# Where the tensors of a two-block transformer kernel begin in SBUF: weight units 64 bytes off multiples of 128

## What is computed

```python
def modulated_residual(x, c, g, w_mod, b_mod, fn):
    shift, scale, gate = ada_params(c, w_mod, b_mod)      # silu(c) @ w_mod + b_mod
    h = rms_norm(x, g) * (1 + scale) + shift
    return x + gate * fn(h)

def swiglu(h, w_gate, w_up, w_down):
    return (jax.nn.silu(h @ w_gate) * (h @ w_up)) @ w_down

def moe_swiglu(h, w_router, w_gate, w_up, w_down):
    logits = jnp.einsum('bsd,de->bse', h, w_router)
    top_val, top_idx = lax.top_k(logits, TOP_K)            # 2 of 8 experts
    top_w = jax.nn.softmax(top_val, axis=-1)
    gates = jnp.sum(jax.nn.one_hot(top_idx, 8) * top_w[..., None], axis=-2)
    for e in range(8):
        out = out + gates[..., e:e + 1] * swiglu(h, w_gate[e], w_up[e], w_down[e])
    return out
```

## The kernel before

| tensor | start mod 128 |
|---|---|
| `x_tokens`, `x_normed`, `hT_high`, `hT_low`, `table` | 0 |
| `act`, `aT_high`, `aT_low`, `gate_bc` | 0 |
| `mod_acc`, `mod_in`, `raw_units`/`units_low`, `units_high` | 0 |
| `router_high_low`, `qkv`, `qkT`, `masks`, `prob`, `moe_sum`, `y_high`, `y_low`, `scatter_hot` | 96 |

## Time and profile before

### The profile page before, as it was taken

One profiled execution on the slowest core, in us unless ns is written; L12 is line 12 of the kernel. 1 busy time (PEld: TensorE's weight loads), 2 busy tenths in 40 slices (PEclk: granted clock), 3 DMA queues, 4 the chain that ended last, 5 costly groups with the idle time before them and its releaser, 6 DMA issues.

```text
span 2088.6 us, 29232 instructions
## 1 busy us (share of the span) xinstructions
PE 1956.6 (94%) x9196; PEld 1613.7 (77%) x9196; DVE 1639.9 (79%) x2173; ACT 1138.5 (55%) x1616; POOL 36.1 (2%) x47
## 2 busy tenths in 40 slices
PE   2999999989899999999999999988899999789998
PEld 1987888867688888888888888766778888677886
DVE  6988886757798888888888989896676669666554
ACT  1434444443677767776776777654444444545443
POOL 2000000000000000000000000000000000000000
PEclk9999999977899999999999999987699999779999
DMA  8867996545599999999999999947368875735662
GB/s 297 328 242 265 342 357 196 146 153 180 188 359 333 359 329 368 328 365 327 349 346 341 354 338 354 346 159 215 120 211 267 272 234 151 238 116 177 213 217 74
DMA packets 368361, 551.08 MB, mean 264 GB/s; under 512 B 35715, under 2 KB 292998, under 8 KB 368230
## 3 DMA queue, kind: packets, MB, share of 16 engines
q1 hardware_dynamic: 365280, 547.81, 77.3%
q10 hardware_dynamic: 2118, 1.46, 0.2%
q0 software_dynamic: 832, 0.30, 0.1%
HBM read 548.39 MB, written 1.08 MB: 263 GB/s over the span
## 4 chain that ended last, share of the span: by engine, by line
PE 83%; DVE 10%; ACT 3%; issue 3%; DMA 1%; POOL 0%; DVEq 0%; ACTq 0%; POOLq 0%
PE ps L401 23%; PE ps L403 23%; PE ps L402 23%; PE ps L877 3%; PE ps L866 2%; DVE units_low L396 2%; PE ps L1046 2%; PE ps L931 2%; DVE mod_acc L1546 1%; PE ps L728 1%; PE ps L854 1%; DVE x_tokens L1573 1%; ACT prob L1239 1%; DVE x_normed L1572 1%; DMA mod_in<-in_mod_w 1%
## 5 line engine op out<-in xcount | busy, mean ns | idle before, releaser
L396 DVE TENSOR_TENSOR units_low<-raw_units,units_high 128x1024 fp32r<-128x1024 f32 (+2 forms) x840 | 983.0, 1220 | 121.9 <-ACT units_high L392 115.7
L392 ACT ACTIVATE units_high<-raw_units 128x1024 fp32r<-128x1024 f32 (+2 forms) x840 | 845.0, 1058 | 244.3 <-PE ps L403 232.8
L401 PE MATMUL ps<-units_high,hT_high 128*128 128x512 f32 (+2 forms) x1576 | 624.1, 396 | 4.3 <-DVE act L1642 2.9
L402 PE MATMUL ps<-units_low,hT_high 128*128 128x512 f32 (+2 forms) x1576 | 621.3, 394 | 0.0
L403 PE MATMUL ps<-units_high,hT_low 128*128 128x512 f32 (+2 forms) x1576 | 621.0, 394 | 0.0
L401 PEld LDWEIGHTS ps<-units_high,hT_high 128*128 128x128 f32 (+1 forms) x1576 | 297.4, 189 | 75.8 <-DVE act L1642 3.6
L403 PEld LDWEIGHTS ps<-units_high,hT_low 128*128 128x128 f32 (+1 forms) x1576 | 297.2, 189 | 68.3
L402 PEld LDWEIGHTS ps<-units_low,hT_high 128*128 128x128 f32 (+1 forms) x1576 | 297.4, 189 | 67.5 <-issue 0.2
L401 PE MATMUL ps<-units_high,aT_high 128*128 128x512 f32 x632 | 259.6, 411 | 1.1 <-DVE qkT L1783 0.6
L403 PE MATMUL ps<-units_high,aT_low 128*128 128x512 f32 x632 | 249.1, 394 | 0.0
L402 PE MATMUL ps<-units_low,aT_high 128*128 128x512 f32 x632 | 248.8, 394 | 0.0
(11 more groups left out here) (273 smaller groups left out, 1486.9 us busy)
## 6 DMA issues: line engine op xcount, KB each, us to landing
raw_units<-in_moe_w_gate SPq DMA_DIRECT2D x352, 256.0 KB, 4.0
raw_units<-in_moe_w_up SPq DMA_DIRECT2D x352, 256.0 KB, 4.7
raw_units<-in_moe_w_down SPq DMA_DIRECT2D x176, 512.0 KB, 4.9
mod_in<-in_mod_w SPq DMA_DIRECT2D x96, 512.0 KB, 5.5
mod_in<-in_w_mod SPq DMA_DIRECT2D x96, 512.0 KB, 5.0
raw_units<-in_w_gu SPq DMA_DIRECT2D x176, 256.0 KB, 3.3
raw_units<-in_w_down SPq DMA_DIRECT2D x44, 512.0 KB, 4.2
raw_units<-in_w_in SPq DMA_DIRECT2D x32, 512.0 KB, 7.2
```

The lines of the kernel that those rows point to most:

```text
L392: eng.activation(whi[:rows, n % H, 0:width], raw[:rows, n % R, 0:width], ACT.Copy).then_inc(f.hi, 1)
L396: eng.tensor_tensor(low[:rows, n % R, 0:width], raw[:rows, n % R, 0:width], whi[:rows, n % H, 0:width].bitcast(F32), ALU.subtract).then_in ...
L401: pe.matmul(dst, ah, bh, start=start, stop=False, **kw)
L402: pe.matmul(dst, ah, bl, start=False, stop=False, **kw)
```

## The change

The change makes `gate_bc` 16 floats (64 bytes) larger and leaves the name for its first 1024 columns. All tensors allocated after it begin 64 bytes later; those before it, `hT`, `act` and `aT` among them, stay. The short ramp is dropped from the table: the first eight columns of the long ramp have the same values, and the stacked identity moves to the columns that it had. The table keeps its width.

```diff
-C_ID, C_ONE, C_LT, C_IO, C_I8, C_FREQ, C_COS, C_SIN = 0, 128, 256, 384, 512, 520, 552, 616
-C_ST = 680
+C_ID, C_ONE, C_LT, C_IO, C_ST, C_FREQ, C_COS, C_SIN = 0, 128, 256, 384, 512, 520, 552, 616
 C_W = 696
+PHASE = 16
...
-    c[:, C_I8:C_I8 + E] = np.arange(E)
...
-    gate_bc = sb("gate_bc", [P, D])
+    gate_room = sb("gate_bc", [P, D + PHASE])
+    gate_bc = gate_room[:, 0:D]
...
-        i8 = table[:, C_I8:C_I8 + E][:, None, :].broadcast_to((P, T, E))
+        i8 = table[:, C_IO:C_IO + E][:, None, :].broadcast_to((P, T, E))
```

## The result

The changed kernel takes 2095.68 us (median of 20 runs, 2092.17 to 2097.01), the kernel before beside it 2091.76 us (20 runs, 2085.69 to 2094.39). The ratio is 1.0024, with a 95% interval of 1.0017 to 1.0032. It is slower, by less than the 0.3% of the forecast's bound but clear of the measurement.

A forecast was written before the change was run, and what follows sets the result against it. The prediction took TensorE to bound the kernel, with the DMA engines close behind in the experts. Its terms summed 0 + 0 + 0 + 0 on 2090.75 us, giving 2091 us, no change, with a range of 2045 to 2120 us.

The forecast's parts named there:

- The bound: Whole kernel: TensorE leads with 83% of the chain of waits; in the experts the DMA engines have a share of 0.99.
- Router, VectorE, ScalarE: Router's table reads, splits and modulation sums: 0 us each, as shapes and waits stay and start places showed no clear cost.
- TensorE's operands: Moving against stationary operand start in 6400 matmuls of 512 columns: between -19 and +12 ns each, taken as 0.
- pair (a): The scatter's matmuls, both operands starting at 96: 233 ns each, read as absolute place costing nothing within about 3 ns.
- The convolution's row: 256-column matmuls with both operands read at 0: 118 ns, against the router's 130 ns with operands at 0 and 96.
- The 19 ns that are no columns: Each 512-column matmul: 232.5 ns from start to start against 213.3 ns for its columns at 2.4 GHz.
- Transfers: Loads of units and mod_in beginning at 64 in place of 0: taken as 0, no surcharge for a start off 128.
- The rows of q10: ScalarE's DMA queue, mostly masks at 96 off 128: 730 MB per percent of engine span against 709 for the main queue.
- The third rival: Dearer transfers in the experts: up to 1% hidden, then 8 us per percent, 2131 us at 6%; chance 0.06.
- would just stay covered: The SwiGLU's stretches, at a DMA share of 0.95, would still hide transfers that were 6% dearer.
- the slower one: Operand reads 64 bytes apart hinder each other more: 3 ns a matmul gives 2110 us, 12 ns 2168 us; chance 0.14.
- The faster one: Operand reads 64 bytes apart hinder each other less: 2068 us for a quarter of 19 ns, 2022 for all; chance 0.30.

The follow-up runs named there:

- e1: The changed kernel with the spare floats behind x_normed, so inputs and units both begin at 64; 2090.82 us, ratio 1.0004 to the kernel before.
- f1: The changed kernel with spare floats set so that units and inputs all begin at multiples of 256; 2058.73 us, ratio 0.985 to the kernel before.
- g1: The changed kernel with 32 spare floats for 16, so inputs and units all begin at 128 modulo 256; 2059.13 us, ratio 0.9859 to the kernel before.
- g3: g1 with only hT_low and aT_low 32 bytes further; 2095.86 us, ratio 1.0028 to the kernel before.

## Why the prediction was wrong

**The bound: right.** TensorE leads, one nanosecond a matmul is 6.4 us, and the transfers in the experts are close behind.

**Router, VectorE, ScalarE: right,** 0 each. L396 went from 1222 to 1221 ns, L392 stayed at 1060, and e1 has the router's edit at no cost.

**TensorE's operands: the step that failed.** I put the term at 0, since the scatter, with both operands at the same place, ran like the rest. It measured +0.8 ns, inside the bounds of -19 to +12, and so 5.1 us in the sum, where I had 0. Two faults lay under it. First, pair (a) has the kernel's shape, but not the relation that the change makes; a row with an unchanged relation can't bound the cost of changing it. Second, I counted places modulo 128 because the change speaks of multiples of 128. The kernel before was not a kernel with both operands at the same place. It had them 128 apart modulo 256, one of the slow places; the change went to another slow place. The convolution's row, read as (0, 0) beside the router's, was 128 apart as well. The 19 ns that are no columns were the hint: 6 of them depend on the place. f1 and g1 show it.

**Transfers: a wrong 0 that cost nothing.** A piece takes 50.5 ns in place of 48.0, 5% more. The Trainium skill, DMA: Bandwidth & Descriptors, section "How a descriptor splits into AXI transactions", gave an estimate of 6% if its rule for reads held for writes. The measured 5% is near it, and the rule's multiple of 256 fits too: in g1 units begin at 128 modulo 256, and a piece takes 50.8 ns. Its count of beats does not fit. By it a piece at 32 would need 33 beats and one at 128 would need 36, estimates of 3% and 12%; the table has 50.5 and 50.8 ns, about the same. Nor is the surcharge equal for each piece: before, 98% of them took exactly 46 ns; after, 43% still do, and most others take 47 to 61. So the runs show the price of a start off a multiple of 256, and its mechanism stays open. The rows of q10 could not see that; its `masks` were off a multiple already and its share is rounded to a fifth. The third rival's size was near and its price was not: I had the time turn at 1% more engine time, and e1, with the dearer pieces and the old operand places, is at 1.0004. In the stretches the share rose only from 0.99 to 1.02 and, in the SwiGLU, from 0.95 to 0.97 (my "would just stay covered" at 6% was itself over 1: 0.95 x 1.06 is 1.007), less than the pieces' 5%; why is not shown. The loads still came in time.

**The rivals.** Of the two on TensorE both were half right: the reads do hinder each other, and the place decides how much. The change got the slower one at a quarter of its smallest price (0.8 ns where I had put 3). The faster one had the size of what f1 gained (2058.7 us; I had 2068 us for a quarter of the 19 ns, and it was 5.8 of them), but at a place where the change didn't go. Its cap on what the experts could gain was too low: f1's experts took 98.3 us where I allowed 99.1, at 354 GB/s for the 350 that I had as full.

**Open:** why 0 and 64 ahead are cheap and 16, 32 and 96 are not, and why one bad pair costs the others time. The runs give the dependence, not the circuit. Places modulo more than 256 were told apart only so far: `hT` and `aT` lie 256 apart modulo 512 in f1, and both settle at 226 and 227 ns.

## What to carry to other kernels

Where TensorE is fed float32r matmuls of 512 columns back to back, try starts of the moving and the stationary operands at the same place modulo 256 bytes; here that alone was worth 1.4% (g1, 128 spare bytes in each partition) to 1.5% (f1). It is not a rule for other shapes: the 256-column products ran slower there. Before calling a layout change neutral, write out the starts of both operands modulo 256 and not only the shift. Starts at multiples of 256 also made the 1 KB packets of the DMAs some 5% shorter. That gave no time here, since TensorE led, and no run shows what it gives where transfers lead.

## What the runs showed of the hardware

- A 512-column float32r matmul takes 226.7 to 234.4 ns from start to start at the 2.4 GHz level by where the moving operand starts relative to the stationary one, modulo 256, with all three lines of a product alike in it. The Trainium skill, SBUF — State Buffer, "Who interferes with whom", has two independent read ports for TensorE; with float32r these runs show that the two reads are not free of each other: with the low stationary operands alone displaced (g3), the matmul beside whose stream they are loaded took 239.1 ns for 226.7.
- The distances settle into fixed patterns (seven long before; 231 and 236, or 233, 233, 234 after; 226 and 227 only at the best place). One kernel can settle into more than one: after the change the experts show both of theirs.
- A 1 KB packet to a start off a multiple of 256 takes 50.3 to 50.8 ns on average in place of 47.7 to 48.1, at 16, 32, 64, 96 and 128 alike.
- A 256-column float32r matmul takes 117.7 ns from start to start after the change, 118.7 before, and 120.0 with both operands at the same place modulo 256 (f1, g1).
